# The sample group's attention, woven into the last 35 blocks of the prompt's attention

## What is computed

```python
# branch A; groups g with (window, dilation) = (128, 1), (512, 4), (2048, 16)
qa, ka, va = parts of h @ w_in          # per group and head; h = normed, modulated x
qa, ka = rmsnorm(qa, q_gain), rmsnorm(ka, k_gain)
# prompt: each query reads the keys 0, d, 2d, ..., window back
s = q @ k.T * 64 ** -0.5 - slope * distance      # -inf where not allowed
m = max(s); p = exp(s - m); l = sum(p); o = p @ v / l; lse = m + log(l)
# sample: the same over 129 positions of [cache, new keys]; cache of 128, 512, 2048 rows
alpha = softmax(lse over the 3 groups); o_a = sum_g alpha_g * o_g
branch_a = (o_a * silu(z_a)) @ w_branch_a
```

## Time and profile before

| | |
|---|---|
| time, median of three runs | 3330.77 us |
| the profiled execution | 3324.52 us |
| its span, first to last instruction | 3322.7 us |
| TensorE busy, of the span | 3010.6 us (91%) |
| VectorE, ScalarE, POOL busy | 1083.0, 976.6, 241.6 us |
| mean granted TensorE clock (1 is 2.4 GHz) | 0.931 |
| DMA, mean over the span | 100 GB/s |

### The profile page before, as it was taken

The page is one execution under the profiler, slowest core; times in us unless marked ns, Lnnn a source line. Parts: engine busy times, 40 slices in busy tenths (PEclk is TensorE's granted clock), DMA queues, the critical chain, the costliest instruction groups (busy, mean ns, idle before and its releaser), DMA issues. The chain is left out here.

```text
span 3322.7 us, 43067 instructions
## 1 busy us (share of the span) xinstructions
PE 3010.6 (91%) x16796; PEld 2653.2 (80%) x16796; DVE 1083.0 (33%) x2826; ACT 976.6 (29%) x1996; POOL 241.6 (7%) x261
## 2 busy tenths in 40 slices
PE   6699999999969999998999999999999836489699
PEld 6578889999969899997888888888888523379699
DVE  1420000111136656553223333333333521233421
ACT  1431111111123333332444444444444312222300
POOL 0000000000022223221000000000000000211000
PEclk7799999999979999999999999999999567689899
DMA  4222212221121222212021222222122289645632
GB/s 154 85 73 73 69 58 110 73 73 67 49 80 60 91 73 98 86 62 66 28 64 50 62 80 76 56 79 81 50 66 89 79 294 399 213 149 156 210 130 85
DMA packets 271717, 331.83 MB, mean 100 GB/s; under 512 B 74592, under 2 KB 219808, under 8 KB 267168
## 3 DMA queue, kind: packets, MB, share of 16 engines
q1 hardware_dynamic: 267808, 312.11, 28.8%
q0 software_dynamic: 2560, 8.39, 0.8%
q10 hardware_dynamic: 1152, 8.65, 0.6%
HBM read 224.14 MB, written 104.94 MB: 99 GB/s over the span
## 5 line engine op out<-in xcount | busy, mean ns | idle before, releaser
L581 PE MATMUL hgrn_u<-h_hi,hgrn_w_hi 128*128 128x424 f32 (+1 forms) x640 | 251.4, 393 | 0.0
L250 PE MATMUL project_acc<-project_v_hi,h_hi 128*128 128x512 f32 x544 | 216.7, 398 | 24.0 <-DVE h_lo L401 24.0
L582 PE MATMUL hgrn_u<-h_lo,hgrn_w_hi 128*128 128x424 f32 (+1 forms) x640 | 228.0, 356 | 0.0
L583 PE MATMUL hgrn_u<-h_hi,hgrn_w_lo 128*128 128x424 f32 (+1 forms) x640 | 227.9, 356 | 0.0
L262 PE MATMUL project_acc<-h_hi,project_w_hi 128*128 128x424 f32 (+1 forms) x640 | 225.9, 353 | 0.0
L264 PE MATMUL project_acc<-h_hi,project_w_lo 128*128 128x424 f32 (+1 forms) x640 | 225.9, 353 | 0.0
L263 PE MATMUL project_acc<-h_lo,project_w_hi 128*128 128x424 f32 (+1 forms) x640 | 225.8, 353 | 0.0
L251 PE MATMUL project_acc<-project_v_lo,h_hi 128*128 128x512 f32 x544 | 215.3, 396 | 0.0
L252 PE MATMUL project_acc<-project_v_hi,h_lo 128*128 128x512 f32 x544 | 215.3, 396 | 0.0
L1099 PE MATMUL attention_u<-h_hi,attention_w_hi_q 128*128 128x424 f32 (+1 forms) x480 | 202.0, 421 | 9.6 <-DVE attention_w_lo_q L1263 9.6
L1209 ACT ACTIVATE attention_probs<-attention_probs,attention_o_out 128x256 f32<-128x256 f32 (+1 forms) x384 | 156.7, 455 | 183.9 <-DVE attention_o_out L1294 183.9
(11 more groups left out here) (212 smaller groups left out, 5894.7 us busy)
## 6 DMA issues: line engine op xcount, KB each, us to landing
sample_v<-in_v_c SPq DMA_DIRECT2D x8, 3328.0 KB
sample_k<-in_kT_c SPq DMA_DIRECT2D x24, 1024.0 KB, 18.6
scratch_values<-project_v_out SPq DMA_DIRECT2D x64, 256.0 KB
scratch_gates<-hgrn_raw SPq DMA_DIRECT2D x64, 212.0 KB, 2.1
merge_gates<-scratch_gates SPq DMA_DIRECT2D x32, 424.0 KB, 3.9
scratch_sums<-attention_o_out SPq DMA_DIRECT2D x48, 264.0 KB, 2.8
attention_rows<-scratch_sums SPq DMA_DIRECT2D x64, 198.0 KB, 3.0
attention_w_raw<-in_w_qkv SPq DMA_DIRECT2D x48, 256.0 KB, 2.8
```

The lines of the kernel that those rows point to most:

```text
L250: pe.matmul(u[:, :], h_hi[:, k, rows], v_hi[g % 2][:, k, :], start=(k == 0), stop=False)
L581: pe.matmul(bank, w_hi[m % 2][:, k, :], h_hi[:, k, c], start=(k == 0), stop=False)
L582: pe.matmul(bank, w_hi[m % 2][:, k, :], h_lo[:, k, c], start=False, stop=False)
L583: mm = pe.matmul(bank, w_lo[m % 2][:, k, :], h_hi[:, k, c], start=False, stop=(k == KD - 1))
```

## The change

`phase_sample` is gone as a stage, and its work is done by `phase_attention`:

- The prologue projects 20 units in place of 10: first the last set (11), whose queries and keys are stored to memory (`store_last`, a new scratch tensor `qk_last`) and loaded again at block 160 (`load_last`); then set 0. `set_at(n)` gives the set that projection stage n makes. Ahead of block 0 come 170 eighths; blocks then carry 5 eighths and, in one of twenty, a sixth (`first_k`), and the 960 are done with block 156 (`THROUGH`).
- From block 157 on `h_hi` and `h_lo` are not read any more, and the sample's buffers are put in their place (`instead`): two buffers for keys of banks 0 and 1, one for banks 2 and 3, two for values. Its PSUM is that of the projections.
- The sample's work of TensorE is cut into 104 parts: S (one bank of scores), T (up to four transposes, one bank for all), W (up to four tiles of weighing), O (turning the output). Three parts go into each step from 160 (`FIRST`) to 194: the first behind `score` and ahead of `weigh`, the others ahead of `turn`. Their VectorE and ScalarE work goes into the same steps' lists.
- Keys and values are loaded by POOL, in step order, the values in four pieces per sequence (64 loads, and 24 small ones of new rows). POOL also does the zeroing, between the first keys and the first values, once the last unit is done. SP loads queries, new keys and tables at step 158 (`load_tables`) behind the last `store_qk`; VectorE waits for all of these in step 159 (`sample_queries`).
- The joins of the last pair have three buffers in place of four of their own.

```diff
-    AHEAD, STEP = 10, 5
+    AHEAD = 10
+    EACH = 3
-        first_k = lambda T: 8 * 10 + AHEAD + STEP * T
+        set_at = lambda n: (n - 1) % SETS
+        first_k = lambda T: 8 * 20 + AHEAD + 101 * T // 20
+        THROUGH = step_of(8 * 10 * SETS - 1)
...
-        rows += [at(f"rows{i}", i, [P, G * 4 * 66], F32) for i in range(4)]
+        rows += [at(f"rows{i}", i, [P, G * 4 * 66], F32) for i in range(2)]
...
+        parts = [("S", 0, c) for c in range(4)]
+        for b in range(SB):
+            for r in range(4):
+                parts += [("T", b, r)] + [("S", b + 1, r)] * (b + 1 < SB) + [("O", b - 1, 0)] * (b > 0 and r == 0)
+            parts += [("W", b, r) for r in range(4)]
+        parts += [("O", SB - 1, 0)]
+        FIRST = THROUGH + 4
+        step_of_part = {x: FIRST + i // EACH for i, x in enumerate(parts)}
...
+        def sample_scores(pe, b, c):
+            if b == 0 and c == 0:
+                pe.wait_ge(s["evac_done"], 10 * SETS)
+                pe.wait_ge(s["sample_q_ready"], 3)
+            wait(pe, s["sample_max_done"], 4 * b + c - 1)
+            pe.wait_ge(k_in[c][b % len(k_sb[c])], 16 * (b // len(k_sb[c]) + 1))
...
             for T in range(STEPS):
+                now = parts_at(T)
                 score(pe, T)
                 for k8 in eighths(T)[:2]:
                     eighth(pe, k8)
+                for x in now[:1]:
+                    sample_part(pe, *x)
                 if T:
                     weigh(pe, T - 1)
...
                 for k8 in eighths(T)[2:]:
                     eighth(pe, k8)
+                for x in now[1:]:
+                    sample_part(pe, *x)
                 turn(pe, T)
...
+        def sample_queries(dve):
+            dve.wait_ge(s["sample_zeroed"], 4)
+            dve.wait_ge(s["sample_q_loaded"], 16 * (G + PAIRS))
...
+            dve.wait_ge(s["sample_q_ready"], 2)
+            dve.wait_ge(s["sample_tables_loaded"], 16 * 3 * PAIRS)
+            dve.sem_inc(s["sample_q_ready"], 1)
...
+        def store_last(sp):
+            for kind in range(2):
+                sp.dma_start(dr["qk_last"][kind], qk[kind][1][:, :]).then_inc(s["last_stored"], 16)
+        def load_last(sp):
+            sp.wait_ge(s["s_done"], 2 * BLK * (SETS - 2))
+            sp.wait_ge(kv_out[1], KV * (SETS // 2 - 1))
+            for kind in range(2):
+                sp.dma_start(qk[kind][1][:, :], dr["qk_last"][kind]).then_inc(s["last_loaded"], 16)
+        def load_tables(sp):
+            for i in range(2):
+                sp.wait_ge(kv_out[i], KV * (SETS // 2))
...
+            sp.wait_ge(s["sample_zeroed"], 4)
...
+                if T == THROUGH + 2:
+                    store_qk(sp, SETS - 1)
+                    load_tables(sp)
+                if T == BLK * (SETS - 2):
+                    load_last(sp)
...
+        def load_sample_keys(pool, b, c):
+            deep = len(k_sb[c])
+            wait(pool, s["sample_s_done"], 4 * (b - deep) + c + 1)
+            w = bank_of_keys(c)
+            pool.dma_start(k_sb[c][b % deep][:, :, :], dr["kT_c"][b, :, :, c * CH:c * CH + w]).then_inc(k_in[c][b % deep], 16)
...
+            for T in range(LAST):
+                for n in at_step(T, 4):
+                    gate_joined(pool, n)
+                if T == THROUGH:
+                    pool.wait_ge(s["unit_done"], 10 * SETS)
+                for b, kind, r in loads_at(T):
+                    if (b, kind, r) == (0, "V", 0):
+                        for x in (q_diag[:, :, :, :], pen[:, :], own[:, :], sel[:, :, :]):
+                            pool.memset(x, 0.0).then_inc(s["sample_zeroed"], 1)
...
         with ExitStack() as ctx:
-            keep(ctx, "oT_s", [P, PAIRS, NS])
-            phase_sample(nc, t, dr)
+            ctx.enter_context(nc.sbuf_tensor("place_of_oT_s", [P, PAIRS, NS], F32))
             phase_merge(nc, t, dr)
```

More of the change, by code:

```diff
@@ L995, in phase_attention @@
     STEPS = SETS * BLK
[L996 removed]
+    AHEAD = 10
+    COLS = 3 * CH + P + 3 * ST
+    GROUP_OF_BANK = (1, 2, 2, 0)
+    W = 32
+    EACH = 3
     h_hi, h_lo = t["h_hi"], t["h_lo"]
@@ L1086, in phase_attention @@
         at_step = lambda T, later: [n for n in range(8 * PAIRS) if begins(n) + later == T]
-        LAST = begins(8 * PAIRS - 1) + 6
+        parts = [("S", 0, c) for c in range(4)]
[6 more added lines that the diff above has]
+        step_of_part = {x: FIRST + i // EACH for i, x in enumerate(parts)}
+        parts_at = lambda T: [x for x in parts if step_of_part[x] == T]
+        of_tiles = lambda r: range(4 * r, min(4 * r + 4, KEYS + 1))
+        tile = lambda j: slice(W * j, W * j + W)
+        bank_cols = lambda c: slice(c * CH, min((c + 1) * CH, COLS))
+        bank_of_keys = lambda c: CH if c < 3 else P
+        LAST = max(begins(8 * PAIRS - 1) + 6, step_of_part[parts[-1]] + 1)
         def eighth(pe, k8):
@@ L1232, in scalar_program @@
                     weights_high(act, n, half)
-            for unit in range(11):
+            for unit in range(21):
                 if unit:
@@ L1236, in scalar_program @@
                 square(act, unit)
[L1237 to L1240, removed]
+                if unit >= 5 and unit % 5 < 2 and unit < 20:
+                    weights_high(act, unit // 5 + 1, unit % 5)
+            for T in range(LAST):
+                if T < STEPS:
+                    weights(act, T)
                 for unit in finished(T - 1):
@@ L1250, in scalar_program @@
                     square(act, unit)
[L1251 to L1256, removed]
+                for kind, b, r in parts_at(T):
+                    if kind == "T":
+                        sample_copy(act, b, r)
+                    if kind == "S" and r == 3:
+                        sample_weights(act, b)
+                if T < STEPS:
+                    copy_turned(act, T)
         def weights_low(dve, n, half):
@@ L1341, in vector_program @@
                     weights_low(dve, n, half)
-            for unit in range(10):
+            for unit in range(20):
                 leave_unit(dve, unit)
-                if unit in (4, 5):
-                    weights_low(dve, 2, unit - 4)
-            for T in range(STEPS):
-                largest(dve, T)
-                if T:
+                if unit >= 4 and unit % 5 in (4, 0) and unit < 19:
+                    weights_low(dve, (unit + 1) // 5 + 1, (unit + 1) % 5)
+            for T in range(LAST):
+                if T < STEPS:
+                    largest(dve, T)
+                if 0 < T <= STEPS:
                     leave_sums(dve, T - 1)
@@ L1462, in sync_program @@
             store_qk(sp, 0)
+            store_last(sp)
+            for n, half in ((3, 1), (4, 0), (4, 1), (5, 0)):
+                load_weights(sp, n, half)
+            store_qk(sp, 1)
             for T in range(STEPS):
```

404 lines of the change are left out of this document (191 added, 213 removed).

## The result

The changed kernel takes 3348.29 us (median of 5 runs, 3345.36 to 3352.75) against 3330.77 before (5 runs, 3328.84 to 3331.79): a ratio of 1.0057, 95% interval 1.0045 to 1.0069. It is slower by 17.5 us, where I had forecast 52 us less. The profiled execution's span is 3350.0 us, 27.3 more than before; the two profiled executions lie 6.3 us under and 3.5 us over the medians, so some 10 us of the 27.3 are spread between executions.

A forecast was written before the change was run, and what follows sets the result against it. Bound by TensorE to block 173, by TensorE at its lower clock to 191, then by DMA. Added 53.4 + 3.3, remaining 56 + 32 x 6.0, less 356.8 removed, gave -52 us: 3279 us, range 3246 to 3325.

The forecast's parts named there:

- ten units and five eighths ahead: Ahead of block 157: ten added projection units before block 0, 53.4 us, and five more eighths in blocks, 3.3 us.
- (a): Blocks 157 to 159, with neither eighths nor sample parts: 3.3 us each, 10 us.
- (b): Wait in block 159 for tables, sample's queries and zeroing, every engine waiting: about 16 us.
- (c): Blocks 160 to 191, three sample parts in each: mean 6.0 us a block.
- (d): Tail behind block 191: joins 26.3 us as before, about 4 for the last batch's parts, 30 us.
- removed: Old stretch from block 157 to the merge stage's first load, sample stage included: 356.8 us taken away.
- rival 2: In blocks 160 to 191 the clock stays at 1.2 GHz: 7.3 us a block, change -10 us; chance 0.14.
- my bound of 2.3: POOL's queue of sample loads: issuing 1 MB takes at most 2.3 us.
- my bounds of 2.6 to 13: Zeroing on POOL at the start: between 2.62 us and 13 us for all 4920 columns.
- rival 3: Blocks 176 to 191: SP's small transfers stand behind POOL's bulk, VectorE waits for rows; change +23 us, chance 0.11.
- rival 1: From block 157 on DMA ends last, loads and block traffic setting the time: change -77 us, chance 0.20.

The follow-up runs named there:

- e5: Changed kernel with joins of pairs 1 and 2 begun 8 and 10 blocks earlier, rows and gates of batches 21 to 23 loaded in block 159: 3306.49 us.
- e9: e5 with batches 24 to 27 of the last pair begun 2, 2, 1 and 1 steps later: 3298.87 us, ratio 0.9901 to the kernel before.
- e2: Changed kernel with all POOL loads but the first sequence's keys held until the tables have landed: 3354.03 us.
- e8: e5 with only the second sequence's keys and values held back until the tables have landed: 3308.62 us.
- e10: e5 with the edits of both e8 and e9: 3299.25 us.
- e4: Changed kernel with the rows of batches 20 to 23 loaded four steps earlier into free buffers, compares left in place: 3325.17 us.
- e12: Changed kernel with only one group's rows in three loaded for batches 20 to 23, all waits kept: 3337.61 us.
- e3: Changed kernel with POOL's loads of values cut into runs of 1 KB, the same bytes: 3353.45 us.
- e6: Changed kernel with the bulk issued by ScalarE one step later in place of POOL, values in runs of 1 KB: 3337.53 us.

## Why the prediction was wrong, by its steps

From the start of block 157 (2538.4) to the merge stage (2860.3), by the stretches of the prediction:

| step | predicted | measured |
|---|---|---|
| ten units and five eighths ahead (block 157 starts later) | 56.7 | 59.5 |
| (a) blocks 157 to 159 | 10 | 13.9 |
| (b) the start | 16 | 36.9 |
| (c) 32 blocks | 32 x 6.0 = 192 | 239.9 |
| (d) tail | 30 | 31.2 |
| removed | -356.8 | -356.8 |
| behind the merge's start | 0 | 2.7 |
| sum | -52 | +27.3 |

The sum is that of the two profiled executions. The added units and the tail were right within 3 us. (a) took 3.9 us more: block 158 took 4.0 us, the two-tile block at the lower clock, and block 157, with the last unit's norm and a join in it, 6.1. The clock of the 32 blocks was as forecast, 0.77, at both levels: rival 2 did not happen. That it is the sample stage's very number is luck, as the stalls are in it; where the joins do not stall it is 0.88 (e5 and e9, 2600 to 2720). POOL issues 1 MB in 0.76 us, below my bound of 2.3, and the zeroing took 4.6 us on POOL (four memsets, 2.68 + 1.52 + 0.22 + 0.14), in my bounds of 2.6 to 13.

**(c) is the step that failed, by rival 3.** The 23 steps other than the eight take 5.07 us each, better than my 6.0: alone that would have given 32 x 5.07 = 162 for the term and -82 for the sum, which no run came near, as the DMA engines decide once the stalls are gone. The eight steps with the compares of batches 20 to 27 take 14.2 each, 73 us more than eight of the others. That is what rival 3 describes, by its own sign: VectorE's compares wait for rows for 53.1 us. The rest of the 73 is mostly steps 184 and 188, 13 us over two others, which wait for no rows: there a join and the next batch's compare stand in one step, and (c), which took VectorE's work by the mean of a block, had no term for that. I gave rival 3 0.11 for three reasons, which the runs correct. I let it begin with block 176, where rows have to be fresh; the rows of batches 20 to 23 had been in memory since block 143, but were asked for only one step ahead, and that one step was the cover of a load of 3.2 us, not of one of 16. I held against it that POOL's backlog runs dry when blocks stall: true, and it is what ends each stall, six times, when rows had been under way for 9 to 16 us. And I priced SP's packets (192 in four blocks), where the shorter queue decides, mostly POOL's. The Trainium skill's rule (DMA: Bandwidth & Descriptors, Queues, rings and completion order), by which each DMA engine takes turns between queues packet by packet, agrees with the 717 to 718 packets above; I cited it and did not follow it into block 164. That rival 3's time (3354) is so near the measured 3348 is luck: it put 171 us on blocks 176 to 191 and 96 on the 16 ahead, and they took 118 and 121.

**(b) failed too, and only in part by the same mechanism.** I let its loads begin 4 us into block 157, with the keys stored; they began at 2578.3, 39.9 us into it. The larger part is the store of the last unit (1 MB), which I had counted from a stage with one queue: beside some 12 MB of a second one it landed after 21.1 us, where the same store took 5.2 in the kernel before. But SP issued that store only at 2556.1, 17.7 us into block 157. It had stood 6.7 us in the issue of another store, and then 5.5 us at a store of joined rows, whose multiplication by the gate had to wait on POOL behind 16.5 us of zeroing and issues of bulk:

```profile
2543.51 6.74 SPq L1597 DMA_DIRECT2D out_v_p<-attention_v  x1
2555.77 0.33 SPq L1662 DMA_DIRECT2D scratch_o_a<-attention_rows  x1
2556.14 0.43 SPq L1606 DMA_DIRECT2D out_kT_p<-attention_kT  x1
```

```profile
SPq L1662 <- POOL attention_rows L1728: 5.5, 1, 5.5
```

From the loads to the first score it then took 10.9 us, not 21.4, and so 10.5 of the 35.9 us by which the loads came late do not show in (b). But (b) did not cost what it measured: e2, e8 and e10 took 14 to 23 us out of it and the time stayed, as the bulk is late instead.

**What decides behind that** is rival 1, the DMA engines. Where the joins don't stall (e5, e9) they are full for 120 us on end, at 0.88 of the clock. In the change they are not, since bulk and blocks take turns: a stall holds the parts that free the buffers, and then the bulk has nothing to load (POOL stands 121.8 us in all in front of loads of keys, until TensorE's scores free their buffers).

Not settled: how much of steps 175 and 180, in e4 and e12, is due to loads of values ahead of the rows in SP's queue, to z, and to the hand-over behind a late compare; no run separates them. Nor is the 2.7 us behind the merge's start explained.

## What to carry to other kernels

When bulk moves onto a second DMA queue, go through every small transfer on the first that an in-order engine waits for, and price its landing as the shorter of the two queues in packets times the other queue's packet (here 45 to 58 of 170 to 310 ns in place of 3 us), not by its bytes or its landing when alone. Look, too, at what stands behind the bulk's issues on the engine that issues it. Then ask for such data that many steps earlier, or move its consumer out of the stretch: that turned 1.0057 into 0.9901 here, with the bulk untouched. A gap that the DMA engines fill with work needed later is not lost time, and closing it gained nothing here (e2, e8, e10).

## What the runs showed of the hardware that was not expected

- With both queues full, SP's small packets and POOL's large ones go one for one (718 to 717 from 2560 to 2570 of the change; 484 to 585 in e12, where SP's queue was not full throughout), so POOL moves 8 to 12 times the bytes.
- Values loaded by POOL in runs of 1 KB (e3) and keys in runs of 2 KB and 512 B all travelled in packets of 4096 B, values in runs of 8 KB (the change) in packets of 8192 B. The same loads from ScalarE's queue (e6) had packets of 1024, 2048 and 512 B.
- ScalarE's issue of a load takes 0.68 us with an empty queue and 2 us on average (14.51 / 7) with loads backed up, and blocks its other work. SP's store above took 6.7 us to issue beside POOL's bulk, where such stores took 0.4 to 1.1 in the kernel before. POOL's issue of a load stays at 0.53 to 0.82 us in the change.
- A memset of 3072 columns takes POOL 2.68 us, as much as VectorE's 2.62.
